# Layer 2 of a six-layer forward pass: the sums of squares of two query or key tiles issued together, behind every second tile

## The reference, cut to what matters

```
proj = h @ w_in
q = apply_partial_rotary(rms_norm(qkv[:, :, 0, g], q_gain[g]), cos, sin)
k = apply_partial_rotary(rms_norm(qkv[:, :, 1, g], k_gain[g]), cos, sin)
o, lse = dilated_window_attention(q, k, qkv[:, :, 2, g], window // dilation, dilation)
```

## Time and profile before

| | |
|---|---|
| median of 3 runs | 3306.97 us (3304.75 to 3308.42) |
| the profiled execution's own time | 3309.21 us |
| its span | 3307.5 us |
| granted TensorE clock, mean over the span | 0.983 |
| busy: PE, weight loads, DVE, ACT, POOL | 96%, 79%, 50%, 33%, 47% |
| second layer, query and key stages | about 440 to 521, 598 to 672, 756 to 830, 914 to 988 us |

### The profile page before, as it was taken

How to read it: one execution, slowest core, us unless ns; L and a number is a source line. 1 busy time by engine, 2 the same in 40 slices (tenths; PEclk the granted TensorE clock), 3 DMA queues, 4 the chain that set the end, 5 groups by cost and what they waited for, 6 DMA issues and landing times.

```text
span 3307.5 us, 39150 instructions
## 1 busy us (share of the span) xinstructions
PE 3184.5 (96%) x16114; PEld 2628.3 (79%) x16114; DVE 1640.6 (50%) x2141; ACT 1100.9 (33%) x1448; POOL 1558.2 (47%) x1138
## 2 busy tenths in 40 slices
PE   6999999999999999999999999989999999989998
PEld 5988878787878788789887877766888877768887
DVE  5763565657574443534636666665212266542223
ACT  3222233434343332232212434444222343242222
POOL 3544466556463454444443511126445565344444
PEclk9999999999999999999999999999999999989999
DMA  4544421122121232245444211112332332122331
GB/s 144 178 166 140 140 100 64 65 67 73 64 76 52 89 102 90 89 128 179 166 140 149 64 51 35 35 40 79 108 98 93 102 128 89 64 64 90 101 100 66
DMA packets 279315, 320.03 MB, mean 97 GB/s; under 512 B 6866, under 2 KB 245089, under 8 KB 278946
## 3 DMA queue, kind: packets, MB, share of 16 engines
q1 hardware_dynamic: 240960, 247.48, 23.3%
q10 hardware_dynamic: 38178, 70.06, 6.3%
HBM read 311.22 MB, written 6.29 MB: 96 GB/s over the span
## 4 chain that ended last, share of the span: by engine, by line
PE 87%; DVE 6%; ACT 3%; POOL 2%; issue 1%; DMA 1%; ACTq 0%; SPq 0%; DVEq 0%; POOLq 0%
PE ps L536 24%; PE ps L538 23%; PE ps L537 23%; PE psx L961 2%; POOL Wl L344 1%; PE psx L733 1%; PE ps L993 1%; PE ps L777 1%; PE psx L711 1%; ACT Wh L1209 1%; PE psx L536 1%; PE psx L537 1%; PE psx L538 1%; PE psx L750 1%; PE psx L627 1%
## 5 line engine op out<-in xcount | busy, mean ns | idle before, releaser
L344 POOL TENSOR_TENSOR Wl<-Wr,Wh 128x512 fp32r<-128x512 f32 x928 | 1276.7, 1407 | 1527.4 <-ACT Wh L1209 1523.2
L536 PE MATMUL ps<-Ah,Wh 128*128 128x512 f32 x1920 | 773.6, 403 | 6.5 <-POOL Wl L344 6.5
L538 PE MATMUL ps<-Ah,Wl 128*128 128x512 f32 x1920 | 749.8, 390 | 0.0
L537 PE MATMUL ps<-Al,Wh 128*128 128x512 f32 x1920 | 749.4, 390 | 0.0
L1209 ACT ACTIVATE Wh<-Wr 128x2048 fp32r<-128x2048 f32 x232 | 442.9, 1909 | 368.2 <-DMA Wr<-in_w_mlp_in_dram 111.4
L536 PEld LDWEIGHTS ps<-Ah,Wh 128*128 128x128 f32 x1920 | 361.5, 188 | 92.4 <-issue 11.1
L536 PE MATMUL ps<-Yh,Wh 128*128 128x512 f32 x1088 | 426.4, 392 | 4.4 <-issue 2.7
L537 PEld LDWEIGHTS ps<-Al,Wh 128*128 128x128 f32 x1920 | 361.6, 188 | 83.5 <-issue 10.3
L537 PE MATMUL ps<-Yl,Wh 128*128 128x512 f32 x1088 | 424.6, 390 | 0.0
L538 PE MATMUL ps<-Yh,Wl 128*128 128x512 f32 x1088 | 424.5, 390 | 0.0
L538 PEld LDWEIGHTS ps<-Ah,Wl 128*128 128x128 f32 x1920 | 361.1, 188 | 76.4
(11 more groups left out here) (401 smaller groups left out, 4111.1 us busy)
## 6 DMA issues: line engine op xcount, KB each, us to landing
Wr<-in_a_w_in_dram SPq DMA_DIRECT2D x48, 1024.0 KB, 6.6
modw<-in_w_mod_dram ACTq DMA_DIRECT2D x96, 512.0 KB, 5.5
Wr<-in_b_w_in_dram SPq DMA_DIRECT2D x40, 1024.0 KB, 5.0
Wr<-in_w_mlp_in_dram SPq DMA_DIRECT2D x32, 1024.0 KB, 5.7
Wr<-in_w_mlp_out_dram SPq DMA_DIRECT2D x32, 1024.0 KB, 5.1
Wr<-in_a_w_out_dram SPq DMA_DIRECT2D x16, 1024.0 KB, 5.2
Wr<-in_c_w_in_dram SPq DMA_DIRECT2D x16, 1024.0 KB, 5.7
Wr<-in_attn_w_qkv_dram SPq DMA_DIRECT2D x12, 1024.0 KB, 5.1
```

What stands on the lines that cost most here:

```text
L344: last = pool.tensor_tensor(E.Wl[:, s, part], E.Wr[:, s, part], E.Wh[:, s, part].bitcast(F32), ALU.subtract)
L536: pe.matmul(o, ah, bh, start=first, stop=False)
L537: pe.matmul(o, ah, bl, start=False, stop=False)
L538: return pe.matmul(o, al, bh, start=False, stop=last)
```

## The change

On PE, nothing is issued behind an odd tile; behind tile t = 2, 4, 6, 8, 10 the sums of the squares of t-2 and t-1 follow one another, and behind the first value tile those of 10 and 11. On ACT the order at an even tile becomes: copy of t, root of t-2, square of t, root of t-1; at an odd tile: square, copy. The PSUM bank of an even tile is free at the square, which is now its last reader. The buffers and their number stay as they were.

```diff
                     for f in range(2):
                         if i or t >= 2:
-                            tile_f(p, f, Ah, Al, (nb + f) % 4, ("B", "qk", i, t), A.of("B", "cp", i, t))
-                        if t:
+                            tile_f(p, f, Ah, Al, (nb + f) % 4, ("B", "qk", i, t), A.of("B", "cp" if t % 2 else "sq", i, t))
+                        if t and t % 2 == 0:
+                            ssq(i, t - 2)
                             ssq(i, t - 1)
                         t += 1
...
                     if g + u == 0:
+                        ssq(i, 10)
                         ssq(i, 11)
...
+        def squared(i, t):
+            if t >= 2:
+                act.wait_ge(*X.of("B", "ssq", i, t - 2))
+            elif i:
+                act.wait_ge(*V.of("B", "y", 0, 2 * (i - 1) + 1))
+            act.activation(sq[:, t % 2, :], ps[t % 4][:], ACT.Square).then_inc(*A.did("B", "sq", i, t))
+
+        def copied(i, t):
+            if t >= 3:
+                act.wait_ge(*V.of("B", "qk", i, t - 3))
+            elif i:
+                act.wait_ge(*X.of("B", "end", i - 1))
+            act.activation(tmp[:, t % 3, :], ps[t % 4][:], ACT.Copy).then_inc(*A.did("B", "cp", i, t))
...
+                        act.wait_ge(*T.of("B", "qk", i, t))
+                        if t % 2 == 0:
+                            copied(i, t)
+                            if t:
+                                sqrt(i, t - 2)
+                        squared(i, t)
+                        if t % 2:
+                            copied(i, t)
+                        elif t:
                             sqrt(i, t - 1)
...
                 if g == 0:
+                    sqrt(i, 10)
                     sqrt(i, 11)
```

More of the change, by code:

```diff
@@ L788, in mixer_b @@
                     if i + t == 0:
-                        first_f("B", p, (0, 1), [("B", "qk", 0, f) for f in range(2)], [A.of("B", "cp", 0, f) for f in range(2)])
+                        first_f("B", p, (0, 1), [("B", "qk", 0, f) for f in range(2)], [A.of("B", "cp" if f else "sq", 0, f) for f in range(2)])
                     for f in range(2):
                         if i or t >= 2:
-                            tile_f(p, f, Ah, Al, (nb + f) % 4, ("B", "qk", i, t), A.of("B", "cp", i, t))
-                        if t:
+                            tile_f(p, f, Ah, Al, (nb + f) % 4, ("B", "qk", i, t), A.of("B", "cp" if t % 2 else "sq", i, t))
+                        if t and t % 2 == 0:
+                            ssq(i, t - 2)
                             ssq(i, t - 1)
@@ L1409, in mixer_b @@
                     for f in range(2):
-                        if t:
-                            sqrt(i, t - 1)
[L1412 to L1423, removed]
+                        act.wait_ge(*T.of("B", "qk", i, t))
[7 more added lines that the diff above has]
+                        elif t:
+                            sqrt(i, t - 1)
                         if f == 0:
```

## The result

The changed kernel took 3324.89 us (median of 5, 3323.29 to 3328.74), the kernel before 3308.42 beside it: ratio 1.0051, 95% interval 1.0036 to 1.0066, so 16.5 us slower. Run again with the experiments it took 3333.80 against 3307.53: ratio 1.0081 (1.0066 to 1.0095), 26 us slower. The forecast was +27.7 us, slower with chance 0.91, range 3316 to 3344. Sign and place were right. In this first profile the loss in the layer itself was smaller than forecast; in the second profile of the same kernel (experiment 7) it came near the forecast, in part by something the forecast doesn't have.

The account below looks back on a forecast made before the run. It took PE to bound the query and key stages; late low parts would make PE stand, net 3 x 7.1 + 6.4 = +27.7 us on 3306.97, giving 3334.7 us. Range for 8 in 10: 3316 to 3344.

Parts of the forecast that it names:

- Bound: Second layer's query and key stages: PE busy 100.00 of 100 us, so changes pay in PE time or cost through PE waits.
- What PE saves: Query and key stages: 0.05 us per pair, 24 pairs, 1.2 us, plus 0.7 at the first sum; about 2 us.
- The rival in which the 0.80 us record is a price and goes: PE's L536 behind sums: the record's whole excess is saved as well, giving 3297 us; chance 0.03.
- The late low part: POOL's L344 behind t-1's late rope: ready at P + 21.9 or 22.8, wanted at 19.86; PE stands 7.2 us a round.
- The rival without a loss: Query and key stages: low parts stay in time and PE only saves its 2 us, 3305 us; chance 0.06.
- the signs named: Profile after: about 20 L536 waits totalling 25 to 30 us, L344 behind second rope, DVE root waits 1 to 2, sums 0.86 apart.
- Its size: Layer's four rounds: 3 x 7.1 + 6.4 = +27.7 us from PE standing for late low parts.
- P: Moment when PE has done an even tile t, P(t); the forecast counts later steps from it, 12.65 us a pair.
- t = 4 to 10: DVE and POOL at these tiles: t-1's reciprocal at P + 8.40, low part from 16.6 to 22.6.
- the 0.2 us from the low part's end to PE's first matmul: PE's restart behind a late panel: 0.2 us allowed for signal and an uncovered weight load.
- The rival with DVE as the bound: DVE: both `rest`s of a pair take 6.62 us, low part 0.9 later; +9, 3344 us; chance 0.11.
- The rival without contention: POOL and DVE: same wait with L344 5.0 and L1990 0.75; low part at P + 20.9, +8.9, 3316 us; chance 0.07.

Follow-up runs that it names:

- experiment 7: The changed kernel unaltered, timed again in the session of its variants: 3333.80 us against 3307.53 for the kernel before.
- experiment 1: Changed kernel with POOL making the panel's low part before the ropes of t-2 and t-1: 3303.75 us against 3306.80 for the kernel before.
- 5: Changed kernel with POOL making the low part between the two ropes of a pair: 3303.96 us against 3307.53 for the kernel before.
- 3: Changed kernel's ACT order with late roots, but PE's old single sums between tiles: 3332.80 us against 3306.80 for the kernel before.
- experiment 2: Kernel before, single sums kept, with POOL making the low part ahead of the rope of t-1: 3308.81 us against 3306.80.

## Why the prediction was right, and where its sizes were off

**Bound.** Right: PE's stage without idle time, and a change there that makes PE wait costs in full.

**What PE saves.** The two sums of a pair run 0.86 us apart, as forecast: the chain after gives them 1.72 us.

```profile
619.56 1.72 PE psx L733 x4
```

The 0.05 us a pair came out as 0.23 us a round against 0.3. The rival in which the 0.80 us record is a price and goes (3297 us) fell with experiment 1.

**The late low part.** Right, and shown by taking it away (1, 5), by making it without the pairs (3), and by doing the POOL move alone (2). The rival without a loss, 3305 us, is what experiment 1 measured (3303.75) once POOL's order was another; with the order of the change it is refuted. Of the signs named, the place of the wait, the second rope ahead of the low part and the distance of the sums came as told; the waits were fewer and shorter, 12 and 20.1 us, not about 20 and 25 to 30, and DVE waited 3.91, 2.63 and 1.60 us for a root behind a pair in round 1, not 1 to 2.

**Its size** is where the sum failed: +22.7 and +26.1 us in the layer in the two profiles, not 27.7, and the second number holds 1.6 us of the lower clock, which the sum doesn't have. That the total came as near as it did is in part luck, since these errors have opposite signs:

- Left out: the table load, +1.04 us at the first wait of the rounds i = 1 to 3. The prediction had ACT's root at P + 1.06 for every even tile. Before, the load was hidden: it ran at 606.64 and the first root waited for its sum until 610.03, since that root stood first in ACT's order of the round.
- Mis-sized: "t = 4 to 10", where I gave `rest` of t-2 6.62 us because its product L1990 lies beside an L344. DVE after, tiles 2 and 3 of round 1 (the product is L2003 there, the reciprocal L1998):

```profile
633.82 3.35 DVE L1998 RECIPROCAL rs<-rs 128x512 f32<-128x512 f32 x1 [0.18 <-ACT rs L1393]
637.21 0.80 DVE L2003 SCALAR_TENSOR_TENSOR KB<-tmp,PK,rs 128x512 f32<-128x512 f32 x1
...
639.63 3.33 DVE L1998 RECIPROCAL rs<-rs 128x512 f32<-128x512 f32 x1
643.00 0.85 DVE L2003 SCALAR_TENSOR_TENSOR KB<-tmp,PK,rs 128x512 f32<-128x512 f32 x1
...
649.45 3.35 DVE L1998 RECIPROCAL rs<-rs 128x512 f32<-128x512 f32 x1 [3.91 <-ACT rs L1393]
...
693.39 1.86 DVE L2003 SCALAR_TENSOR_TENSOR KB<-tmp,PK,rs 128x512 f32<-128x512 f32 x1
```

This `rest` took 639.63 - 633.82 = 5.81 us, though its product lay beside an L344 (636.13 to 642.04). The low part for tile 8 was done at 653.03, where P(4) = 632.04: P + 21.0, not 22.6, and with P(6) late already it was in time. Of these 1.6 us about 0.6 come from the `rest` and 1.0 from the low part itself, which took 5.02 us and not 6.0, since DVE stood waiting for its next root. From P(2) to tile 14, round 1 gave 77.05 us against 78.4 forecast: tile 6 at 22.7 (forecast 21.9), tile 10 at P(6) + 21.7 and the second value panel at P(10) + 21.4 (forecast 22.8 both), and no wait at tiles 8 and 12 (0.9 each forecast). In the first round, +4.98 against 6.4. In the second profile, where a product did take 2.03 us, tile 10 started at P(6) + 23.0, beyond the forecast's 22.8: the price was no constant.

A third term was small: the 0.2 us from the low part's end to PE's first matmul had no row behind it. It was 0.06 (642.04 to 642.10), and the tile behind it took 5.6 us and not the 5.44 of the sum.

**The rival with DVE as the bound** is wrong: the DVE rows above show it waiting 3.91 us for the next root after a pair, and experiment 1 has it keep up with a PE that never stands. The rival without contention (+8.9) is wrong too, though it held for one panel: the low part for tile 8 took 5.02 us and was in time, but those for tiles 6 and 10 took 5.91 and 5.96 and the loss was +22.7.

## What to carry to other kernels

When results are handed on in pairs, the second of each pair is late by one full step of the consumer, however small the saving at the producer; follow that lateness through every in-order queue to whatever is queued behind it. Here the victim, a panel's low part, had nothing to do with the pair: it only stood behind it on POOL, with 2.9 to 4.0 us to spare, and at P(2) it came 6.7 us later (P + 15.97 before, P + 22.65 after, of which 1.04 is the table). The cure is to put work with its own deadline in front of work that waits, and the look for it starts with the spare time of each queued step, not with the busy shares.

## What the runs showed of the hardware

- **Contention between DVE and POOL comes by instruction.** L344 is four instructions of 1.255 us each (5.02 / 4). The product L2003 took 0.75 us beside an idle POOL. In three rows where it was held beside an L344, it ended 0.63 or 0.64 us behind the end of the running one, which is where the next one started: from 637.21 it took 0.80, with the second L344 from 637.38; from 693.39 it took 1.86, with the fourth from 694.61; and before, from 626.84 it took 1.62, with the third from 627.82. POOL is held in turn: the L344 that starts inside such a product takes 1.77 us in place of 1.26. The third of the group from 636.13 took 1.70, beside the rotary product (L2012, 32 rows), which also has two inputs in SBUF. So a low part took about 5.02 us where neither kind of product held it, 5.5 where one did and 5.9 to 6.0 where two did; the prediction put the whole 0.95 us down to the product L1990.
- **A product that waits can be passed over more than once.** In the second profile of the changed kernel one took 2.03 us, from 486.82, across two L344 instructions. In experiment 2 one waited through the rest of a whole group, and POOL lost nothing:

```profile
463.14 5.03 POOL L344 TENSOR_TENSOR Wl<-Wr,Wh 128x512 fp32r<-128x512 f32 x4
```

```profile
463.95 4.77 DVE L1990 SCALAR_TENSOR_TENSOR QB<-tmp,PK,rs 128x512 f32<-128x512 f32 x1
```

So the 1.62 us that the prediction took for the product beside an L344 was one point between 0.75 and 4.77, set by where the product falls. Why it was passed over in these two is not shown. All this was read from the traces, not tested by a kernel of its own; it would explain why the same order gives rounds of 163.59 and 164.10. The Trainium skill (SBUF — State Buffer, section Who interferes with whom) calls the shared port pair an exclusive lock, and says that a VectorE instruction with two SBUF inputs contends with a GpSimd instruction that reads SBUF; that the lock is held for the whole instruction it says of VectorE's 2-port modes. The three held rows agree with the lock, and show the whole-instruction hold for two SBUF inputs too.
- **A wait can be followed by the lower clock.** Of the 48 waits for L344 in the layer in the four profiles that have them, two, of 3.01 and 2.64 us, were followed by some 3 us at the lower level, at 1.6 us each; others of 2.63 to 2.70 us were not. What decides it was not tested.
- **A load of ACT's table takes 1.28 us but cost the first root 1.04 us**, and whether it costs anything is set by what ACT waits for behind it.
- **The part of the kernel behind the layer varies by up to 8.6 us between profiled executions** (2213.3 to 2221.9) with the same instructions; the granted clock of the 320 us shown was 0.97 in one and 0.99 in another, the lower level being half of the 2.4 GHz. The times of one kernel go with the clock: of the 21 executions of the kernel before that were timed beside experiment 1, the fastest (3300.48 us) had a mean clock of 0.986 and the slowest (3312.78) 0.982. That the clock is all of the 8.6 us is not shown.
